# Spreading attention's head weights over all 128 rows, and moving one low split on VectorE

## What is computed

```python
    outs = jnp.stack(outs, axis=0)
    wts = jax.nn.softmax(jnp.stack(lses, axis=0), axis=0)
    merged = jnp.sum(wts[..., None] * outs, axis=0)
...
        merged = (jax.nn.sigmoid(ga) * jnp.einsum('bsc,cd->bsd', a, w_att_out[l])
                  + jax.nn.sigmoid(gp) * jnp.einsum('bsc,cd->bsd', p, w_pool_out[l]))
        h = h + jnp.einsum('bsd,de->bse', merged, w_out[l])
```

## Time and profile before

| | us |
|---|---|
| median of 3 runs | 1371.46 (1371.29 to 1372.83) |
| the profiled execution | 1374.04 |
| its span, first to last instruction | 1371.9 |
| TensorE busy | 1298.2 (95%) |
| VectorE busy | 648.1 (47%) |
| ScalarE busy | 383.7 (28%) |
| GpSimd busy | 260.0 (19%) |
| mean granted TensorE clock | 0.977 of full speed |

### The profile page before, as it was taken

The page is one execution under the profiler, slowest core; times in us unless marked ns, Lnnn a source line. Parts: engine busy times, 40 slices in busy tenths (PEclk is TensorE's granted clock), DMA queues, the critical chain, the costliest instruction groups (busy, mean ns, idle before and its releaser), DMA issues.

```text
span 1371.9 us, 17687 instructions
## 1 busy us (share of the span) xinstructions
PE 1298.2 (95%) x7351; PEld 991.7 (72%) x7351; DVE 648.1 (47%) x786; ACT 383.7 (28%) x485; POOL 260.0 (19%) x241
## 2 busy tenths in 40 slices
PE   6999999999999999999998999999989879979987
PEld 5888878877878888888885888777867745534443
DVE  4322543356466365473656532227763436433335
ACT  4222455443242132221325332223221400000002
POOL 1410000002021020120200000273342023323220
PEclk9999999999999999999999999999999979999999
DMA  6523333442425345253431222224015879999995
GB/s 251 184 94 105 99 132 113 168 165 93 153 96 223 112 184 215 95 217 146 183 130 64 92 92 95 90 92 140 2 37 210 346 291 415 415 416 417 417 389 207
DMA packets 45846, 253.32 MB, mean 185 GB/s; under 512 B 10220, under 2 KB 10876, under 8 KB 19154
## 3 DMA queue, kind: packets, MB, share of 16 engines
q1 hardware_dynamic: 36802, 227.94, 43.8%
q0 software_dynamic: 7024, 17.07, 3.4%
q10 hardware_dynamic: 1952, 7.34, 1.4%
HBM read 240.52 MB, written 20.99 MB: 191 GB/s over the span
## 4 chain that ended last, share of the span: by engine, by line
PE 81%; DMA 6%; DVE 5%; issue 3%; ACT 2%; POOL 1%; SPq 1%; POOLq 0%; DVEq 0%
PE ps L371 22%; PE ps L372 21%; PE ps L373 21%; PE ps L2265 5%; DMA experts<-in_w_exp 4%; PE ps L2283 3%; PE ps L2100 1%; DVE experts L1303 1%; PE ps L2253 1%; SPq L616 1%; DMA arena<-h,arena 1%; PE ps L1837 1%; PE ps L2344 1%; PE ps L2349 1%; DMA y<-arena 1%
## 5 line engine op out<-in xcount | busy, mean ns | idle before, releaser
L356 DVE TENSOR_TENSOR w_low<-raw,w_high 128x2048 fp32r<-128x2048 f32 x81 | 214.4, 2647 | 277.7 <-ACT w_high L352 277.6
L371 PE MATMUL ps<-u_high,w_high 128*128 128x512 f32 (+1 forms) x712 | 278.9, 392 | 1.8 <-DVE u_low L339 1.8
L372 PE MATMUL ps<-u_low,w_high 128*128 128x512 f32 (+1 forms) x712 | 277.2, 389 | 0.0
L373 PE MATMUL ps<-u_high,w_low 128*128 128x512 f32 (+1 forms) x712 | 277.2, 389 | 0.0
L352 ACT ACTIVATE w_high<-raw 128x2048 fp32r<-128x2048 f32 x81 | 154.8, 1911 | 186.7 <-PE ps L373 158.3
L371 PEld LDWEIGHTS ps<-u_high,w_high 128*128 128x128 f32 (+1 forms) x712 | 132.9, 187 | 32.7 <-issue 4.0
L373 PEld LDWEIGHTS ps<-u_high,w_low 128*128 128x128 f32 (+1 forms) x712 | 132.9, 187 | 28.8
L372 PEld LDWEIGHTS ps<-u_low,w_high 128*128 128x128 f32 (+1 forms) x712 | 132.9, 187 | 28.2 <-issue 0.2
L371 PE MATMUL ps<-w_high,v_high 128*128 128x512 f32 x320 | 125.2, 391 | 2.8 <-POOL v_low L1678 2.8
L372 PE MATMUL ps<-w_low,v_high 128*128 128x512 f32 x320 | 124.5, 389 | 0.0
L373 PE MATMUL ps<-w_high,v_low 128*128 128x512 f32 x320 | 124.5, 389 | 0.0
(11 more groups left out here) (394 smaller groups left out, 1726.6 us busy)
## 6 DMA issues: line engine op xcount, KB each, us to landing
raw<-in_w SPq DMA_DIRECT2D x82, 1024.0 KB, 4.9
experts<-in_w_exp SPq DMA_DIRECT2D x69, 1024.0 KB, 23.2
arena<-in_w_exp SPq DMA_DIRECT2D x30, 1024.0 KB, 23.8
arena<-in_w_ada SPq DMA_DIRECT2D x24, 1024.0 KB, 5.0
y<-experts ACTq DMA_DIRECT2D x4, 1024.0 KB, 4.5
gates<-arena POOLq DMA_DIRECT2D x16, 256.0 KB, 2.3
arena<-gates POOLq DMA_DIRECT2D x2, 2048.0 KB, 8.8
arena<-y SPq DMA_DIRECT2D x8, 512.0 KB, 6.6
```

What stands on the lines that cost most here:

```text
L356: dve.tensor_tensor(WL[:, 1 - s, :], RAW[:, 1 - s, :], WH[:, 1 - s, :].bitcast(F32), ALU.subtract).then_inc(lo_ready, 1)
L371: pe.matmul(out, a[0], b[0], start=start, stop=False)
L372: pe.matmul(out, a[0], b[1], start=False, stop=False)
L373: return pe.matmul(out, a[1], b[0], start=False, stop=stop)
```

## The change

WROW becomes 128 rows high. VectorE clears it once, before it waits for the statistics of attention, and copies the 12 rows into its top; the copy waits for the clearing. The six products of `weight_rows` take all 128 rows of the identity's column and of WROW, where the 116 further rows are zero in both for the rows selected (the identity has its only one in a row below 12). Their number, width and length stay.

On VectorE the low split of unit F0 moves ahead of `att_gate(1)`.

```diff
@@ -138,7 +138,7 @@
-        WROW = ar(20480, 512, 12)
+        WROW = ar(20480, 512)
...
@@ -1051,6 +1051,7 @@
                     if tile % 2:
                         lo(dve, E0 + tile // 2 + 2)
 
+            link.inc(dve.memset(WROW, 0.0))
             dve.wait_ge(stat, 1)
             dve.tensor_copy(RW[0:32, :], PS[0:32, 0, :]).then_inc(stat, 1)
...
@@ -1068,7 +1069,8 @@
             lo(dve, E0 + 8)
             dve.wait_ge(stat, 8)
-            dve.tensor_copy(WROW, PS[0:12, 2, :]).then_inc(stat, 1)
+            link.wait()
+            dve.tensor_copy(WROW[0:12, :], PS[0:12, 2, :]).then_inc(stat, 1)
             lo(dve, E0 + 9)
...
@@ -1116,8 +1118,8 @@
             pool_gate(3)
             att_gate(0)
+            lo(dve, F0)
             att_gate(1)
-            lo(dve, F0)
             for k in range(4):
                 branch_low(k)
...
@@ -1891,7 +1893,7 @@
                 for g in range(3):
                     for hh in range(2):
                         row = 4 * g + 2 * q + hh
-                        last = pe.matmul(PS[64 * hh:64 * hh + 64, 3 + g, :], IDN[0:12, row:row + 1].broadcast_to([12, 64]), WROW,
+                        last = pe.matmul(PS[64 * hh:64 * hh + 64, 3 + g, :], IDN[:, row:row + 1].broadcast_to([P, 64]), WROW,
                                          start=True, stop=True)
```

## The result

| | before | after |
|---|---|---|
| median of 12 executions, us | 1372.39 | 1369.56 |
| lowest and highest, us | 1371.29, 1375.45 | 1368.41, 1371.82 |
| the profiled execution: time, span, us | 1374.04, 1371.9 | 1369.56, 1367.6 |

The ratio is 0.998, with an interval of 0.9971 to 0.9989: 2.8 us faster, between 1.5 and 4.0. The forecast was 1366.7 us. The side was right, the size was not. The two profiled executions stand 4.5 us apart, which is more than the medians do, and that difference turns out to be the key.

The account below looks back on a forecast made before the run. TensorE, busy nearly the whole span, was taken as the bound. Bursts' clock -3.41, moved split -0.55 and idle-time clock -1.71 gave -5.67 us; less 0.9 allowance, -4.8, or 1366.7 us; range 1364.8 to 1370.2, about 0.85.

Parts of the forecast that it names:

- Direct cost of the 128-row products: TensorE's two weight-spreading bursts: no added time over 128 rows, ends -0.1 and +0.1 us.
- Rival E: Weight-spreading bursts: over all rows the column halves no longer overlap, +5.2 us, total 1372.8 or 1376 us; chance 0.05.
- The clock kept by rows of zeros: Behind both bursts: 128 rows, mostly zeros, remove two half-rate stretches, -3.41 us, other end 0.
- The rival taken from the Trainium skill: TensorE's clock: idle gaps lower it, not rows, so both burst falls stay; 0 instead of -3.41 us; within a 0.18 chance.
- Rival C: Bursts: zero rows don't keep the clock, or rows were never the cause; 1369.2 to 1370.9 us; chance 0.18.
- the third fall: TensorE's half-rate stretch after the idle time ahead of F0: goes as idle shrinks to about 1.3 us, -1.71 us, or 0.
- The row against it: At 944.81 us, 2.81 us of 32-row products without a fall, counted against rows as the cause.
- The meeting on VectorE and GpSimd: At the merge ahead of F0: split and GpSimd addition exclude each other, leaving -0.55 of 1.6 us; bounds -1.6 and +0.95.
- rival D: At the merge: GpSimd gets in first at 320.9, split waits, +0.95 us, total 1369.8 us; chance 0.05.
- rival B: The bursts' falls go, the one ahead of F0 stays after 1.3 us of idle; 1368.4 us; chance 0.22.
- The size of the clock terms: Both bursts and the idle time ahead of F0: three half-rate stretches removed, -3.41 and -1.71 us.
- the allowance: Whole kernel: half a clock fall, 0.9 us, taken off the gain because other executions can have fewer falls.

Follow-up runs that it names:

- the long burst: Changed kernel with each burst's products run four times over: 1384.63 us over 128 rows, 1403.64 us over 12 rows.
- the probe: Changed kernel, each burst made into fourteen: 1590.42 us (12 rows), 1570.48 (128), 1592.77 (32). For idle time: fourteen waits of 1.84 us ahead of each burst instead.
- the table: Ten profiles of before, changed kernel and each part alone, listing clock falls at both bursts and the idle time ahead of F0; 51.72 to 57.20 us across these places.
- that version: Kernel before with only the products over 128 rows, low split of F0 at its old place: 1371.77 us, ratio 0.9992 (0.9981 to 1.0002).
- the last comparison: Changed kernel again, 1370.61 us, and with TensorE waiting for each low half where first read, 1368.42 us, against 23 executions of before, median 1373.48 us.

## Why the prediction was right, and where it was not

**Direct cost of the 128-row products: right.** Forecast 0, measured 0.43 us a step in the long burst, and 2.79 us a burst, as over 12 rows. The two column halves overlap as in the row that stood for it. Rival E, by which they no longer would, is out.

**The clearing: right.** It took 0.49 us at 250.7 us (forecast 0.5), where VectorE was idle anyway.

**The clock kept by rows of zeros: right in its mechanism.** No fall in 38 bursts over 128 rows (28 in the probe, ten in the table), nor in the long ones; 19 in 38 over 12 rows. The rival taken from the Trainium skill ("TensorE: Matmul & The Clock Gate", section "HAM oscillation — how this bites in real kernels"), that idle time is what lowers the clock, is out as far as the bursts go: in the long burst over 12 rows the clock fell while TensorE was busy throughout. Rival C, by which rows of zeros don't keep the clock or rows were never the cause, is out with it. The section's own case has waits of some 3 to 5 us, so the third fall, after 1.84 us, agrees with it in kind but not in length, which the prediction left unsaid. The row against it, 32-row products that went by without a fall, weighed too much in my text: one case without a fall says little where half of the cases have none.

**The meeting on VectorE and GpSimd: right, and in size.** Forecast 4.3 us for the addition on GpSimd, about 2.2 for L1104, 0.55 us won and about 1.3 left; measured 4.31, 2.18, 0.64 and 1.20. The split came 0.23 or 0.24 us before GpSimd in each profile with the moved split; rival D didn't occur. Nor did rival B, that the third fall stays.

**The size of the clock terms: wrong.** The failed step is the allowance: "As an allowance I take off half a fall, 0.9 us". I summed three falls at 1.71 us as the profiled execution of before has them, 5.1 us, and took off half a one. For that one execution the sum is good: 5.67 us forecast, 5.47 measured at the three places, the difference being mostly that a fall costs 1.6 us and not 1.71. But the kernel before does not have three falls in each execution. Its four profiles show 3, 2, 1 and 3. With 0.63 us for the moved split and 1.61 for a fall, the two measurements, 2.8 us (1.5 to 4.0) and 1.9 us (0.4 to 3.6), stand for 1.3 falls (0.5 to 2.1) and 0.8 (up to 1.8). The allowance left 2.5. By the probes before has 2 x 13/28 falls behind the bursts and 2/28 at the idle time, 1.0 in all, which makes the change worth 2.2 us. By the table it is 2 x 0.6 and 0.7, 1.9 falls and 3.7 us, which lies within the first interval and just outside the second. The profiled executions of before may be slow ones by chance: their mean is 1374.2 us, that of its 77 others on record 1373.1. The 5.67 us and the 4.8 after the allowance are outside both intervals. About half of the 5.67 us was not there to be won in a typical execution.

The signs were in view. The falls stood at unlike distances behind the two bursts (0.16 and 1.09 us behind the ends in the earlier trace rows; the prediction counts from the ends of its windows), and the profiled execution was 2.6 us above the median. I wrote both down, and then took off only a third of what the second number said. The whole 2.6 us would have given 1368.4 us, 3.1 below the median of three. That median was itself low, 0.9 us under the median of twelve. The measured 1369.56 us lies within the stated range of 1364.8 to 1370.2, but in the part that belonged to rivals C and D, neither of which occurred; that the range held is luck. The Trainium skill ("TensorE: Matmul & The Clock Gate", section "What's actually happening") calls the moment at which the clock first rises run-variable for one and the same kernel; the falls here agree in kind, with four profiles of before showing three patterns.

**What stays open.** The share of executions with a fall ahead of F0 is 5 in 7 in place and 2 in 28 in the probe; no run decides between them, and so the number of falls in a mean execution of before stays between about 1 and 2. What decides in one execution whether a burst is followed by a fall is not shown either. Each part's own worth isn't resolved by times: 1.1 us by ratio for either, with intervals that take in zero; for the rows the evidence is the clock, not the time of that version. The falls further on (between the blocks, in the mixture of experts) shift in every execution. In the changed kernel, whose two profiles take the same 51.7 us at the three places, they make the scatter; in the kernel before the three places vary by 3.2 us over the four profiles and the rest by 2.0.

## What to carry to other kernels

Look at the granted clock behind bursts of products over few rows, not only behind idle time: where such a burst lasts some microseconds, filling its operands to 128 rows with zeros cost nothing on TensorE here (one memset of 0.49 us on VectorE, in idle time) and took the falls away. A fall in one profile is one draw: before its full price goes into a sum, profile a second execution, or take off all by which the profiled time exceeds the median. Compare the spread of the times too, not only the medians. When an operation moves into an idle time of VectorE, look at what GpSimd does there; two operations that each read two SBUF tiles ran one after the other here, which left 0.64 us of an estimated 1.6.

## What was new about the hardware

- TensorE's clock fell from 1.00 to 0.50 in the midst of uninterrupted 12-row products, 4.4 us after they began, and stayed there for 17.1 us, until other work over 128 rows had run for 5 us; over 128 rows with 116 of zeros it never fell.
- 12 and 32 rows behaved alike: 13 falls in 28 bursts each, in probes of the same rhythm.
- Float32 products of 64 columns over 12 rows and over 128 took the same time: 2.79 us for six pairs of records.
- One fall cost 1.6 us at each of the three places: 3.41 us of work at half rate, seen as 53.98 against 52.36 us between the same two instructions.
- Twelve executions of one unchanged program spread over 5.5 us (1371.86 to 1377.32), and 52 others lie in two groups with nothing between 1372.07 and 1373.21 us. The falls of the clock explain it in part. The mean clock of an execution does not resolve them: worked out from it and the span in the last comparison, before stood at half rate for 57.0 us in the mean of 23 (standard error 1.2) and the changed kernel for 55.0 in the mean of 12 (0.9).
